# A two-layer hybrid trunk on one core: the first tile of each passage between stages in two halves, and the second tile's sum on VectorE

## What is computed

```python
def rms_norm(x, g, eps=NORM_EPS):
    xf = x.astype(jnp.float32)
    y = xf * lax.rsqrt(jnp.mean(xf * xf, axis=-1, keepdims=True) + eps)
    return (y * g.astype(jnp.float32)).astype(x.dtype)

def sq_relu_mlp(x, w_in, w_out):
    return jnp.square(jax.nn.relu(x @ w_in)) @ w_out
...
    for layer in range(DEPTH):
        hn = rms_norm(h, norm_mix_pre[layer])
        if layer % 2 == 0:
            ...
            m = mixer_ab(hn, ab_w_in[e], ab_w_out[e], ...)
        else:
            ...
            m = mixer_ret(hn, ret_w_in[o], ret_w_out[o], pos)
        h = h + rms_norm(m, norm_mix_post[layer])
        f = sq_relu_mlp(rms_norm(h, norm_ffn_pre[layer]), ffn_w_in[layer], ffn_w_out[layer])
        h = h + rms_norm(f, norm_ffn_post[layer])
    return h
```

## Time and profile before

| | us |
|---|---|
| runs of before | 1574.06, 1574.16 (median), 1574.80 |
| profiled execution, its own time | 1574.69 |
| its span | 1572.9 |
| PE busy | 1489.6 |
| DVE busy | 830.7 |
| ACT busy | 498.9 |
| POOL busy | 81.7 |

### The profile page before, as it was taken

The page is one execution under the profiler, slowest core; times in us unless marked ns, Lnnn a source line. Parts: engine busy times, 40 slices in busy tenths (PEclk is TensorE's granted clock), DMA queues, the critical chain, the costliest instruction groups (busy, mean ns, idle before and its releaser), DMA issues.

```text
span 1572.9 us, 23172 instructions
## 1 busy us (share of the span) xinstructions
PE 1489.6 (95%) x10408; PEld 1241.8 (79%) x10408; DVE 830.7 (53%) x1023; ACT 498.9 (32%) x557; POOL 81.7 (5%) x73
## 2 busy tenths in 40 slices
PE   6779999999899999999899999999998999999996
PEld 5567787868688888888788888888887888888885
DVE  5647566574673544445574645555346635354443
ACT  5343434442332222222334242332244312122220
POOL 1000000000210000000110000000003000000001
PEclk9889999999799999999899999999999999999998
DMA  4101212020032323223221313222221322323321
GB/s 174 54 16 34 68 34 68 3 81 31 27 134 94 107 81 107 99 89 108 79 83 54 108 54 104 84 70 92 80 81 54 108 97 90 108 83 105 106 82 54
DMA packets 19299, 125.10 MB, mean 80 GB/s; under 512 B 2240, under 2 KB 2240, under 8 KB 5120
## 3 DMA queue, kind: packets, MB, share of 16 engines
q1 hardware_dynamic: 18800, 121.23, 22.4%
q0 software_dynamic: 400, 2.39, 0.4%
HBM read 121.51 MB, written 2.10 MB: 79 GB/s over the span
## 4 chain that ended last, share of the span: by engine, by line
PE 86%; DVE 6%; ACT 4%; issue 2%; DMA 2%; POOL 1%; POOLq 0%; SPq 0%; DVEq 0%
PE bank L305 22%; PE bank L311 22%; PE bank L308 22%; PE bank L568 7%; PE bank L1123 2%; PE bank L1120 2%; PE bank L1126 2%; DMA raw<-weights 2%; PE bank L319 2%; ACT WH L272 1%; DVE WL L278 1%; PE bank L1155 1%; PE bank L1156 1%; PE bank L1154 1%; PE bank L576 1%
## 5 line engine op out<-in xcount | busy, mean ns | idle before, releaser
L305 PE MATMUL bank<-XH,WH 128*128 128x512 f32 x944 | 380.2, 403 | 32.0 <-DVE WL L278 18.9
L308 PE MATMUL bank<-XL,WH 128*128 128x512 f32 x944 | 373.4, 396 | 0.0
L311 PE MATMUL bank<-XH,WL 128*128 128x512 f32 x944 | 373.3, 395 | 0.0
L278 DVE TENSOR_TENSOR WL<-raw,WH 128x2048 fp32r<-128x2048 f32 (+1 forms) x113 | 254.4, 2252 | 154.2 <-ACT WH L272 154.2
L272 ACT ACTIVATE WH<-raw 128x2048 fp32r<-128x2048 f32 (+1 forms) x113 | 212.2, 1878 | 310.3 <-DMA raw<-weights 310.3
L305 PEld LDWEIGHTS bank<-XH,WH 128*128 128x128 f32 x944 | 181.3, 192 | 73.5 <-issue 30.8
L311 PEld LDWEIGHTS bank<-XH,WL 128*128 128x128 f32 x944 | 180.7, 191 | 38.9
L308 PEld LDWEIGHTS bank<-XL,WH 128*128 128x128 f32 x944 | 181.2, 192 | 38.2 <-issue 1.4
L305 PE MATMUL bank<-AH,WH 128*128 128x512 f32 x512 | 199.4, 389 | 0.4 <-DVE AL L524 0.4
L311 PE MATMUL bank<-AH,WL 128*128 128x512 f32 x512 | 199.2, 389 | 0.0
L308 PE MATMUL bank<-AL,WH 128*128 128x512 f32 x512 | 199.2, 389 | 0.0
(11 more groups left out here) (269 smaller groups left out, 1780.8 us busy)
## 6 DMA issues: line engine op xcount, KB each, us to landing
raw<-weights SPq DMA_DIRECT2D x109, 1024.0 KB, 4.9
h<-x_fm SPq DMA_DIRECT2D x4, 512.0 KB, 7.0
raw<-weights SPq DMA_DIRECT2D x4, 512.0 KB, 3.8
out_fm<-h SPq DMA_DIRECT2D x8, 256.0 KB, 2.0
rc<-ret_const POOLq DMA_DIRECT2D x1, 1536.0 KB, 6.9
pp<-pairs POOLq DMA_DIRECT2D x4, 199.0 KB, 3.8
cst<-const SPq DMA_DIRECT2D x1, 577.0 KB, 10.1
vec<-vectors SPq DMA_DIRECT2D x1, 41.5 KB, 1.9
```

The costliest lines, as they stand in the source:

```text
L278: nc.vector.tensor_tensor(WL[i][:, :n], raw[i][:, :n], WH[i][:, :n], ALU.subtract).then_inc(S("w_lo"), 1)
L305: mm = pe.matmul(bank[b][:], wh, xh, start=(k == 0), stop=False)
L308: mm = pe.matmul(bank[b][:], wh, xl, start=False, stop=False)
L311: mm = pe.matmul(bank[b][:], wl, xh, start=False, stop=(k == len(xs) - 1))
```

## The change

The first tile of each passage is handled in two halves of 256 tokens on DVE, ACT and PE. PE multiplies the high part of a half by both weight parts before it waits for the low part of that half; in each of the four banks the tile is now six products of 256 columns in place of three of 512. The sum h + hn of the second tile (kt = 1) is made on DVE, and POOL's additions begin with kt = 3; after the last block (m == 3) POOL still adds all odd tiles. The retention's first units (banks 0, 1, 6, 7) change as the MLPs' do. `skip_group_check` is an argument for the build alone.

```diff
--- before.py
+++ after.py
@@ -302,15 +302,43 @@
                 for b, w in zip(banks, ws):
                     wh, wl = w[k]
                     first = k == (part[0] if part else 0) and b == banks[0]
-                    mm = pe.matmul(bank[b][:], wh, xh, start=(k == 0), stop=False)
+                    skip = part is not None
+                    mm = pe.matmul(bank[b][:], wh, xh, start=(k == 0), stop=False, skip_group_check=skip)
                     if first and left > 0:
                         mm.then_inc(S("chunk_left"), 1)
-                    mm = pe.matmul(bank[b][:], wh, xl, start=False, stop=False)
+                    mm = pe.matmul(bank[b][:], wh, xl, start=False, stop=False, skip_group_check=skip)
                     if first and left > 1:
                         mm.then_inc(S("chunk_left"), 1)
-                    mm = pe.matmul(bank[b][:], wl, xh, start=False, stop=(k == len(xs) - 1))
+                    mm = pe.matmul(bank[b][:], wl, xh, start=False, stop=(k == len(xs) - 1), skip_group_check=skip)
                     if k == len(xs) - 1:
                         mm.then_inc(S(f"acc_full{b}"), 1)
+
+
+
+        HALVES = (slice(0, T // 2), slice(T // 2, T))
+
+        def first_tile(pe, use, banks, ws, m):
+            for b in banks:
+                n = use.next(b)
+                if n > 1:
+                    pe.wait_ge(S(f"acc_free{b}"), n - 1)
+            for i, tok in enumerate(HALVES):
+                if i == 0:
+                    pe.wait_ge(S("x_first_hi"), m)
+                else:
+                    pe.wait_ge(S("x_hi"), m * KT + 1)
+                for b, w in zip(banks, ws):
+                    wh, wl = w[0]
+                    mm = pe.matmul(bank[b][:, tok], wh, XH[:, 0, tok], start=(i == 0), stop=False, skip_group_check=True)
+                    if i == 0 and b == banks[0]:
+                        mm.then_inc(S("chunk_left"), 1)
+                    pe.matmul(bank[b][:, tok], wl, XH[:, 0, tok], start=False, stop=False, skip_group_check=True)
+                if i == 0:
+                    pe.wait_ge(S("x_first_lo"), m)
+                else:
+                    pe.wait_ge(S("x_lo"), m * KT + 1)
+                for b, w in zip(banks, ws):
+                    pe.matmul(bank[b][:, tok], w[0][0], XL[:, 0, tok], start=False, stop=False, skip_group_check=True)
 
 
 
@@ -363,14 +391,25 @@
         def h_is_ready(eng, m, kt):
             eng.wait_ge(S("h_odd" if kt % 2 else "h_even"), m * KT // 2 + kt // 2 + 1)
 
+        def first_tile_act(act, m, layer, kind):
+            one, two = HALVES
+            act.wait_ge(S("h_first"), m)
+            nc.scalar.activation(XH[:, 0, one], h[:, 0, one], ACT.Copy,
+                                 scale=gain(layer, kind, 0)).then_inc(S("x_first_hi"), 1)
+            h_is_ready(act, m - 1, 0)
+            nc.scalar.activation(XH[:, 0, two], h[:, 0, two], ACT.Copy, scale=gain(layer, kind, 0)).then_inc(S("x_hi"), 1)
+
         def pre_tiles_act(act, m, layer, kind, kts=range(KT)):
             for kt in kts:
-                if m:
+                if m and kt == 0:
+                    first_tile_act(act, m, layer, kind)
+                elif m:
                     h_is_ready(act, m - 1, kt)
                 elif kt % 2 == 0:
                     act.wait_ge(S(f"x_loaded{kt // 2}"), 16)
-                nc.scalar.activation(XH[:, kt, :], h[:, kt, :], ACT.Copy,
-                                     scale=gain(layer, kind, kt)).then_inc(S("x_hi"), 1)
+                if kt or not m:
+                    nc.scalar.activation(XH[:, kt, :], h[:, kt, :], ACT.Copy,
+                                         scale=gain(layer, kind, kt)).then_inc(S("x_hi"), 1)
                 nc.scalar.activation(sq[:, kt, :], h[:, kt, :], ACT.Square).then_inc(S("hsq"), 1)
 
         def pre_root_act(act, m):
@@ -428,24 +467,47 @@
 
 
 
+        def post_term(dve, post, kt, tok=slice(0, T)):
+            return nc.vector.scalar_tensor_tensor(hn[:, kt % 2, tok], f[:, kt, tok], gain(*post, kt), bank[5][:, tok],
+                                                  ALU.mult, ALU.mult)
+
         def residual_dve(dve, m, post, pre=None):
             dve.wait_ge(S("post_root"), m + 1)
             nc.vector.reciprocal(post_rstd, post_root).then_inc(S("post_rstd"), 1)
             dve.wait_ge(S("post_spread"), m + 1)
-            for kt in range(KT + 1):
+            if pre:
+                one, two = HALVES
+                g = gain(*pre, 0)
+                post_term(dve, post, 0, one).then_inc(S("post_first"), 1)
+                dve.wait_ge(S("post_first"), m + 1)
+                nc.vector.tensor_tensor(h[:, 0, one], h[:, 0, one], hn[:, 0, one], ALU.add).then_inc(S("h_first"), 1)
+                post_term(dve, post, 0, two).then_inc(S("post_term"), 1)
+                dve.wait_ge(S("post_term"), m * KT + 1)
+                nc.vector.tensor_tensor(h[:, 0, two], h[:, 0, two], hn[:, 0, two], ALU.add).then_inc(S("h_even"), 1)
+                post_term(dve, post, 1).then_inc(S("post_term"), 1)
+                dve.wait_ge(S("x_first_hi"), m + 1)
+                nc.vector.scalar_tensor_tensor(XL[:, 0, one], h[:, 0, one], g, XH[:, 0, one],
+                                               ALU.mult, ALU.subtract).then_inc(S("x_first_lo"), 1)
+                dve.wait_ge(S("post_term"), m * KT + 2)
+                add_to_h(nc.vector, 1)
+                dve.wait_ge(S("x_hi"), (m + 1) * KT + 1)
+                nc.vector.scalar_tensor_tensor(XL[:, 0, two], h[:, 0, two], g, XH[:, 0, two],
+                                               ALU.mult, ALU.subtract).then_inc(S("x_lo"), 1)
+            for kt in range(2 if pre else 0, KT + 1):
                 if kt < KT:
                     if kt >= 2:
                         h_is_ready(dve, m, kt - 2)
-                    nc.vector.scalar_tensor_tensor(hn[:, kt % 2, :], f[:, kt, :], gain(*post, kt),
-                                                   bank[5][:], ALU.mult, ALU.mult).then_inc(S("post_term"), 1)
+                    post_term(dve, post, kt).then_inc(S("post_term"), 1)
                     if kt % 2 == 0:
                         dve.wait_ge(S("post_term"), m * KT + kt + 1)
                         add_to_h(nc.vector, kt)
                 if kt and pre:
                     x_low(dve, m + 1, *pre, kt - 1)
 
+
+
         def residual_pool(pool, m):
-            for kt in range(1, KT, 2):
+            for kt in range(1 if m == 3 else 3, KT, 2):
                 pool.wait_ge(S("post_term"), m * KT + kt + 1)
                 add_to_h(nc.gpsimd, kt)
 
@@ -472,7 +534,8 @@
                         chunk_ready(pe, cj + 1)
                         ws = [columns(cj + k // 2, k % 2) for k in range(4)]
                         ready = x_tiles(pe, m)
-                        units(pe, use, range(4), ws, X, 1, ready, (0, 6))
+                        first_tile(pe, use, range(4), ws, m)
+                        units(pe, use, range(4), ws, X, 0, ready, (1, 6))
                         pre_sums_pe(pe, m)
                         units(pe, use, range(4), ws, X, 0, ready, (6, 7))
                         pre_spread_pe(pe, m)
@@ -1092,7 +1155,8 @@
                 if hd == 0:
                     chunk_ready(pe, c + 1)
                     ready = x_tiles(pe, m)
-                    units(pe, use, [0, 1, 6, 7], cols, X, 1, ready, (0, 6))
+                    first_tile(pe, use, [0, 1, 6, 7], cols, m)
+                    units(pe, use, [0, 1, 6, 7], cols, X, 0, ready, (1, 6))
                     pre_sums_pe(pe, m)
                     units(pe, use, [0, 1, 6, 7], cols, X, 0, ready, (6, 7))
                     pre_spread_pe(pe, m)
```

## The result

The changed kernel takes 1576.8 us (median of 16 runs) against 1573.9 us (16 runs of before): ratio 1.0024, 95% interval 1.0016 to 1.0033, so slower by 0.24% and clear of no change. One of the 16 runs was a slow one, 2200.5 us at a mean granted clock of 0.637, and is left out of the ratio. The forecast was 1577.4 us. The profiled execution took 1576.19 us.

A forecast was written before the change was run, and what follows sets the result against it. PE, busy in 95% of the 1572.9 us span, was taken as the bound. Falls of the clock less earlier sums gave +2.6 us in two passages and +0.35 in the third, together +3.0: 1577.4 us, range 1572.2 to 1580.3.

The forecast's parts named there:

- PE's start: PE's first product of a passage comes +1.6 us behind the first term instead of +4.17, 2.6 us earlier.
- DVE's queue: DVE's eleven instructions up to the fourth tile's term take 5.8 us, 0.2 less; its last sum moves from +22.55 to +22.35.
- Arrival and pause: PE reaches the sums of squares at +20.7 and stands until +22.4, some 2 us; earlier sums gain 0.9, 0.9 and 0.2 us.
- The clock: Behind the pause at the sums the granted clock falls in all three passages, costing 2.2 us each, between 1.65 and 2.8.
- Sum: Over the three passages: +2.6 us for first and second, +0.35 for the third, together +3.0 us, 0.2% slower.
- the clock that does not fall: The wait moves to the sums without a fall there, or with one in one passage: 1572.2 or 1570.5 us; chance 0.18.
- the faster chain of tiles: POOL holds DVE up less, so sums come 1 us or more earlier per passage: 1566.4 to 1571 us; chance 0.07.
- dearer halves: Halves cost DVE more than taken, sums come 0.3 to 0.8 us later per passage: 1578.3 to 1579.8 us; chance 0.13.

The follow-up runs named there:

- e_halves_only: The changed kernel with the sum of the second tile back on POOL, so the halves alone: 1578.4 us, ratio 1.0028 to before.
- e_fill: The changed kernel with ten more products of 512 columns per passage in front of the sums of squares, into a bank nobody reads: 1573.4 us.
- e_sums_later: The kernel before with DVE's low part of a weight chunk put ahead of its three sums, so the sums come later: 1590.5 us, ratio 1.0100.
- e_late_sums: The changed kernel with the sums of squares behind the seventh tile instead of the sixth, and the factor's spread inside the eighth: 1565.4 us.
- e_sums_early: The changed kernel with two of DVE's three sum additions ahead of its last XL and POOL's first ahead of its last addition to h: 1573.0 us.

## Why the prediction was right

- **PE's start** at +1.6: measured +1.62 (ACT's half XH 0.51, DVE's halves 0.48 and 0.42).
- **DVE's queue**: fourth term expected at +5.8, measured +5.80; last sum expected at +22.35, measured +22.40. The four extra instructions are paid by the undisturbed XL; e_halves_only shows the other side of it, with XL disturbed and the sum at +22.8.
- **Arrival and pause**: expected at +20.7 or some tenths sooner, measured +20.3 in the first passage and +20.8 in the others; PE waits until +22.45. That the second passage repeats the first holds before the change and no longer behind it. The difference at the sums' start is -0.85, -0.84 and -0.17 us for an expected -0.9, -0.9, -0.2.
- **The clock**: a fall in all three passages, as forecast. e_fill shows the fall to be the pause's doing, e_sums_later that a pause brings it without the change. The price was taken as 2.2 us between 1.65 and 2.8, since the pause is much longer than 0.3 us. It was 3.2 us in the first (0.77 in the sums, 2.40 in the seventh tile; 3.3 with the eighth) and 1.7 in each of the others, no more than the pause of 0.3 us had cost before. The average is the 2.2 that was taken, but no passage had it: that the sum fits so well is luck. The upper bound was too low, since the clock was down for some 6.6 us and not 5.5. That is an estimate: the 5.27 us of the seventh tile at 0.50, and 2 x (1 - 0.73) of the 2.5 us of the sums, whose one-column products slow down too.
- **Sum**: +3.0 expected, +3.06 in the passages, +2.9 between the medians; the interval of the ratio is +2.5 to +5.2 us. By passage it was +2.41, +0.82 and -0.17 us for an expected +1.3, +1.3 and +0.35, so the errors cancelled.
- **Rivals**: the clock that does not fall is what e_fill comes near to (1573.4 us, with one fall left); the faster chain of tiles did not come about, nor did dearer halves (the last sum at +22.40 excludes both).

The change is made of parts that gain 6.8 us and a queue position that turned them into a loss of 2.9.

## What to carry to other kernels

Before an engine's start is moved forward, look for the next thing for which it waits, and how far behind it arrives there: here it was 0.75 us in two passages and nothing in the third, and that was the most that an earlier start could give while the sums came no sooner. On TensorE a short pause can cost more than its length, because the clock falls behind it: 0.3 us cost 1.7 us more in the third passage of before. It did so in front of one-column products; 0.29 us in front of products of 512 columns cost no fall in e_late_sums. A pause of 2 us in front of a stretch of narrow products is best spent on the work that stands behind it, here by one tile's products. An idle gap of VectorE was not free while GpSimd was busy in it: in e_sums_early an addition took 1.78 us there and 0.68 alone.

## What the runs showed of the hardware

Two effects were larger than I had thought. Products of one column slow down with the clock as wide ones do: 0.215 us each in place of 0.106 (e_sums_later and before, first passage), and 0.43 for 0.23 with 512 columns (the change, first passage). A DVE addition with both inputs in SBUF took 1.6 to 1.8 us beside a POOL addition, against 0.69 alone, and the disturbed half XL 1.50 against 0.48. SBUF — State Buffer in the Trainium skill (SBUF: two separate sides) calls the port pair of the two engines an exclusive lock held for the whole instruction. These rows agree: in e_halves_only POOL's addition began at 415.25 and ended at 416.71, and the half XL that began at 415.48 ended only at 416.98. The head of the kernel, whose code is the same, took 411.4 to 416.5 us in twelve profiles; its stretches at the lower clock are not the same from one to the next, and whether that is the whole cause stays open.
